# RWKV stage: the inverse's transposed copy by VectorE's 32x32 block transposes; keys, values and outputs turned as 128x128 blocks

## What is computed

```
r, k, v, z, wd, ad = split(token_shift(x @ w_in))
decay = exp(-exp(-softplus(-(w0 + tanh(wd) @ w_up)) - 0.5));  a = sigmoid(a0 + ad @ a_up)
kk = normalize(k * k_k);  k = k * (1 + (a - 1) * k_a)
for t:  sa = S @ a_t                       # a_t = -kk, b_t = kk * a
        S  = S * decay_t + sa b_t^T + v_t k_t^T
        o_t = S @ r_t
o = (o - mean(o)) * rsqrt(var(o) + eps) * gn_w + gn_b      # per head
o = (o + sum(r * k * r_k) * v) * silu(z)
```

## Time and profile before

| what | value |
|---|---|
| median of 3 runs | 3392.51 us |
| the profiled execution: its own time, its span | 3388.05 us, 3386.3 us |
| TensorE busy over the span | 97% |
| VectorE, ScalarE, GpSimd busy over the span | 47%, 21%, 62% |
| RWKV pairs: first matmul of AB of pair 1 to that of pair 8 | 93.2 us to 720.0 us: 89.5 us a pair |

### The profile page before, as it was taken

The page is one execution under the profiler, slowest core; times in us unless marked ns, Lnnn a source line. Parts: engine busy times, 40 slices in busy tenths (PEclk is TensorE's granted clock), DMA queues, the critical chain, the costliest instruction groups (busy, mean ns, idle before and its releaser), DMA issues.

```text
span 3386.3 us, 63178 instructions
## 1 busy us (share of the span) xinstructions
PE 3300.8 (97%) x21442; PEld 2638.0 (78%) x21442; DVE 1576.8 (47%) x3108; ACT 706.2 (21%) x1284; POOL 2092.9 (62%) x3460
## 2 busy tenths in 40 slices
PE   8999999999999989899999999999999999999899
PEld 6777777777788868678877777887887888888687
DVE  3455444446576763581156677223443344323500
ACT  2111111102323220140024445111121112111300
POOL 6444444446677758778763343788666666666565
PEclk9999999999999989999999999999999999999999
DMA  4111111112222213223321111333222222222232
GB/s 147 46 51 46 51 51 45 51 48 75 70 71 74 74 44 93 84 75 93 93 75 38 37 37 38 93 93 93 73 74 80 78 71 74 81 77 76 59 112 87
DMA packets 459581, 239.46 MB, mean 71 GB/s; under 512 B 27901, under 2 KB 456120, under 8 KB 458936
## 3 DMA queue, kind: packets, MB, share of 16 engines
q1 hardware_dynamic: 455656, 232.19, 23.6%
q10 hardware_dynamic: 3792, 5.28, 0.4%
HBM read 233.22 MB, written 4.19 MB: 70 GB/s over the span
## 4 chain that ended last, share of the span: by engine, by line
PE 88%; DVE 7%; ACT 2%; issue 2%; SPq 1%; DMA 0%; DVEq 0%; ACTq 0%; PEldq 0%
PE proj L338 23%; PE proj L339 21%; PE proj L340 21%; PE work L2388 2%; PE work L1136 1%; PE work L674 1%; PE work L1983 1%; PE work L688 1%; PE work L682 1%; ACT hg_tmp L1185 1%; PE work L338 1%; PE work L648 1%; PE work L340 1%; PE work L339 1%; PE work L657 1%
## 5 line engine op out<-in xcount | busy, mean ns | idle before, releaser
L314 POOL TENSOR_SCALAR w_hi<-raw_weights 128x256 fp32r<-128x256 f32 x1728 | 753.8, 462 | 1270.2 <-DMA raw_weights<-w_in 504.6
L318 POOL TENSOR_TENSOR w_lo<-raw_weights,w_hi 128x256 fp32r<-128x256 f32 x1728 | 1354.8, 814 | 0.0
L338 PE MATMUL proj<-x_hi,w_hi 128*128 128x512 f32 x2976 | 1228.1, 413 | 18.5 <-DVE x_lo L1619 6.7
L340 PE MATMUL proj<-x_hi,w_lo 128*128 128x512 f32 x2976 | 1180.8, 397 | 0.0
L339 PE MATMUL proj<-x_lo,w_hi 128*128 128x512 f32 x2976 | 1180.8, 397 | 0.0
L338 PEld LDWEIGHTS proj<-x_hi,w_hi 128*128 128x128 f32 x2976 | 562.2, 189 | 172.1 <-issue 34.5
L340 PEld LDWEIGHTS proj<-x_hi,w_lo 128*128 128x128 f32 x2976 | 561.3, 189 | 137.4
L339 PEld LDWEIGHTS proj<-x_lo,w_hi 128*128 128x128 f32 x2976 | 563.2, 189 | 117.8 <-issue 2.2
L338 PE MATMUL proj<-o_hi,w_hi 128*128 128x512 f32 x256 | 102.3, 400 | 3.7 <-DVE o_lo L1045 3.3
L339 PE MATMUL proj<-o_lo,w_hi 128*128 128x512 f32 x256 | 101.6, 397 | 0.0
L340 PE MATMUL proj<-o_hi,w_lo 128*128 128x512 f32 x256 | 101.6, 397 | 0.0
(11 more groups left out here) (470 smaller groups left out, 4226.7 us busy)
## 6 DMA issues: line engine op xcount, KB each, us to landing
raw_weights<-w_in SPq DMA_DIRECT2D x260, 256.0 KB, 3.1
raw_weights<-b_w_in SPq DMA_DIRECT2D x256, 256.0 KB, 3.1
raw_weights<-a_w_in SPq DMA_DIRECT2D x100, 256.0 KB, 3.2
raw_weights<-w_out SPq DMA_DIRECT2D x64, 256.0 KB, 3.0
raw_weights<-a_w_out SPq DMA_DIRECT2D x64, 256.0 KB, 3.0
raw_weights<-b_w_out SPq DMA_DIRECT2D x64, 256.0 KB, 3.0
raw_weights<-a_w_kv_up SPq DMA_DIRECT2D x32, 256.0 KB, 2.8
mix<-x SPq DMA_DIRECT2D x4, 1024.0 KB, 7.9
```

Of the source, the lines that this page charges most:

```text
L314: pool.tensor_scalar(part(hi_v, s, q), part(raw_v, s, q), 1.0, 1.0, ALU.mult, ALU.mult).then_inc(hi_done, 1)
L318: pool.tensor_tensor(part(lo_v, s, q), part(raw_v, s, q), part(hi_v, s, q).bitcast(F32), ALU.subtract).then_inc(w_split, 1)
L338: pe.matmul(out, w_h, a_h, start=start, stop=False)
L340: return pe.matmul(out, w_l, a_h, start=False, stop=stop)
```

## The change

Four things, in every pair:

- The turn T0 and the blocks G are gone from TensorE. VectorE instead makes `tri` as the 32x32 block transposes of `tri_t` (step T1 before the levels, and T2 to T16 after each level's X, lines 921 and 939 of the new file). Up to that point the inverse has nothing outside its 32x32 diagonal blocks. The four half-width adds of G go too.
- Bs, Vs, Ks (in this order) and `back` are turned as four 128x128 transposes each, instead of sixteen 64x64 matmuls. That leaves two quarters of each block on the other head's partitions, so ScalarE copies each turned bank out in four copies of 64x256, quarters put in place (`turn_heads`). The three turns come right behind AK, and the 3 steps and 1 step around them become 4 steps behind them.
- `back` also goes through ScalarE. VectorE's tail is two operations instead of three: scale and add the bonus in one, bias and gate in the next. The factor 0.5 moves into halved parameters.
- The shift of the next pair's V tile moves ahead of that tail, to the end of the preparation; ScalarE takes the V tile before it squares the output. VectorE's `zz` (gate) comes behind Y2, and ScalarE's `tz` behind its three turns.

```diff
-            yield 3
-            for name, src, bank, free in (("Vs", sh[:, V_], 3, "mB0"), ("Ks", k_s, 1, "mB1"), ("Bs", b_s, 0, "mK0")):
+            for name, src, bank, free in (("Bs", b_s, 0, "mK0"), ("Vs", sh[:, V_], 3, "mB0"), ("Ks", k_s, 1, "mB1")):
                 need(RW_DVE, free)
-                hold()
-                for c in range(NC_R):
-                    for hs in HEADS:
-                        mm = pe.matmul(work[bank][hs, c64(c)], src[hs, c64(c)], ident[hs, hs], start=True, stop=True)
+                for b in range(TB):
+                    mm = pe.transpose(work[bank][:, pair_cols(b)], src[:, pair_cols(b)], ident)
                 mm.then_inc(RW_PE.mark(name), 1)
-            need(RW_DVE, "tt2")
...
-            mm.then_inc(RW_PE.mark("T0"), 1)
-            yield 1
-
-            need(RW_ACT, "T0")
+            yield 4
+
+            need(RW_ACT, "Bs")
             for m in LEVELS:
-                if m > 2:
-                    need(RW_DVE, f"T{m // 2}")
+                need(RW_DVE, f"T{m // 2}")
...
-                for c in range(NC_R if m < LEVELS[-1] else 0):
-                    for hs in HEADS:
-                        even, _ = halves(y_m[hs, c64(c)], m)
-                        mm = pe.matmul(work[1][hs, c32(c)], tri_t[hs, c64(c)], even, start=True, stop=True)
...
+        def turn_heads(act, dst, bank):
+
+            for q in range(2):
+                for h in range(2):
+                    ins = act.activation(dst.rearrange("p (b q d) -> p b q d", q=2, d=64)[HEADS[h], :, q],
+                                         work[bank][:, :].rearrange("p (b h d) -> p b h d", h=2, d=64)[HEADS[q], :, h],
+                                         ACT.Copy)
+            return ins
...
+            chain()
+            done(dve.transpose(tri, tri_t), "T1")
             run(shift(dve, p, Z_, RW_DVE, "z"))
...
-            need(RW_PE, "back")
-            done(dve.tensor_scalar(g_out, work[0][:, :], p1("gn_w", p), p1("gn_b", p), ALU.mult, ALU.add), "o1")
-            chain()
-            done(dve.tensor_tensor(g_out, g_out, bonus, ALU.add), "o2")
+            need(RW_ACT, "back")
+            done(dve.scalar_tensor_tensor(g_out, g_out, h1("gn_w", p), bonus, ALU.mult, ALU.add), "o1")
```

More of the change, by code:

```diff
@@ L538, in build @@
         PR_ACT = steps("prep_act", "lora ta tw sq einc eneg eexc")
-        PR_DVE = steps("prep_dve", "d_k s_k kx d_r s_r a lw kt km L rk Lx ss " + RSQRT + " rsx K kkn kka B ends A R")
-        RW_PE = steps("rw_pe", "AB0 AB1 AK0 AK1 Vs Ks Bs T0 " + lv("Y{0} G{0} X{0}").replace(f" G{LEVELS[-1]}", "") + " " +
+        PR_DVE = steps("prep_dve", "d_k s_k kx d_r s_r a lw kt km L rk Lx ss " + RSQRT + " rsx K kkn kka B ends A R d_v s_v")
+        RW_PE = steps("rw_pe", "AB0 AB1 AK0 AK1 Bs Vs Ks " + lv("Y{0} X{0}") + " " +
                       ch("AS{0} U{0} S{0} O{0}", NC_R - 1) + " AS7 U7 O7 back")
-        RW_ACT = steps("rw_act", "tz Vs Ks Bs T0 " + " ".join(f"Sd{c}" for c in range(1, NC_R - 1)) + " gsq")
-        RW_DVE = steps("rw_dve", "d_v s_v bv mB0 mB1 mK0 mK1 tt1 tt2 d_z s_z zz " + lv("Y{0} T{0} X{0}").replace(f" T{LEVELS[-1]}", "") + " " +
+        RW_ACT = steps("rw_act", "Bs Vs Ks tz " + " ".join(f"Sd{c}" for c in range(1, NC_R - 1)) + " gsq back")
+        RW_DVE = steps("rw_dve", "bv mB0 mB1 mK0 mK1 tt1 tt2 T1 d_z s_z " +
+                       lv("Y{0} X{0} T{0}").replace("Y2", "Y2 zz").replace(f" T{LEVELS[-1]}", "") + " " +
                        ch("AS{0} U{0} S{0}", NC_R - 1) + " AS7 U7 gmean gcen gvar gvar2 " + tagged("g_") +
-                       " on o1 o2 out")
+                       " on o1 out")
         LORA_DVE = steps("lora_dve", "zero_y d s")
@@ L695, in rwkv_chunks_pe @@
             hold = lambda: pe.sem_inc(pe_waited, 1)
+            need(RW_ACT, "Ks")
             need(RW_DVE, f"X{LEVELS[-1]}")
@@ L730, in rwkv_chunks_pe @@
             need(RW_DVE, "on")
[L731 to L734, removed]
+            for b in range(TB):
+                mm = pe.transpose(work[0][:, pair_cols(b)], g_cen[:, pair_cols(b)], ident)
             mm.then_inc(RW_PE.mark("back"), 1)
@@ L755, in rwkv_act @@
                 take_tiles(i + 1, (R_, K_))
-                rwkv_chunks_act(act, i, rwkv_prep_act(act, i + 1))
-                take_tiles(i + 1, (V_, Z_))
+                for _ in rwkv_chunks_act(act, i, rwkv_prep_act(act, i + 1)):
+                    take_tiles(i + 1, (V_,))
+                take_tiles(i + 1, (Z_,))
             rwkv_within_act(act, PAIRS - 1)
-            rwkv_chunks_act(act, PAIRS - 1, iter(()))
+            run(rwkv_chunks_act(act, PAIRS - 1, iter(())))
             stage_end(act, 2, [(RW_ACT.sem, RW_ACT.after(PAIRS))])
@@ L778, in rwkv_prep_act @@
             act.activation(e_exc, e_exc, ACT.Exp).then_inc(PR_ACT.mark("eexc"), 1)
+        def turn_heads(act, dst, bank):
[5 more added lines that the diff above has]
+            return ins
         def rwkv_within_act(act, p):
             need = lambda steps, name: act.wait_ge(steps.sem, steps.done(name, p))
[L782 to L785, removed]
+            for name, dst, bank in (("Bs", b_t[:, :], 0), ("Vs", v_t[:, :], 3), ("Ks", k_t[:, :], 1)):
                 need(RW_PE, name)
-                act.activation(dst, work[bank][:, :], ACT.Copy).then_inc(RW_ACT.mark(name), 1)
+                turn_heads(act, dst, bank).then_inc(RW_ACT.mark(name), 1)
+            need(RW_DVE, "s_z")
+            act.activation(gate, sh[:, Z_], ACT.Tanh, scale=0.5).then_inc(RW_ACT.mark("tz"), 1)
         def rwkv_chunks_act(act, p, prep):
@@ L799, in rwkv_chunks_act @@
             run(prep)
+            yield
             need(RW_DVE, "gcen")
             act.activation(g_sq, g_cen, ACT.Square).then_inc(RW_ACT.mark("gsq"), 1)
+            need(RW_PE, "back")
+            turn_heads(act, g_out, 0).then_inc(RW_ACT.mark("back"), 1)
         PREP_PE_AT = (1, 3, 5, 6)
@@ L866, in rwkv_prep_dve @@
             chain()
-            done(dve.scalar_tensor_tensor(rk, sh[:, R_], p1("r_k", p), k_mod, ALU.mult, ALU.mult), "rk")
+            done(dve.scalar_tensor_tensor(rk, sh[:, R_], h1("r_k", p), k_mod, ALU.mult, ALU.mult), "rk")
             yield
@@ L898, in rwkv_prep_dve @@
             done(dve.tensor_tensor(ar[:, :, 1, :], tokens(sh[:, R_], 64), tokens(e_inc, 64), ALU.mult), "R")
+            yield
+            yield from shift(dve, p, V_, PR_DVE, "v")
         def rwkv_within_dve(dve, p):
@@ L904, in rwkv_within_dve @@
             dve.wait_ge(PR_DVE.sem, PR_DVE.after(p + 1))
-            run(shift(dve, p, V_, RW_DVE, "v"))
             need(PR_PE, "bonus")
@@ L921, in rwkv_within_dve @@
                                    repeat(c_rwkv[:, CR_EYE:CR_EYE + 64], NC_R), ALU.add), "tt2")
+            chain()
+            done(dve.transpose(tri, tri_t), "T1")
             run(shift(dve, p, Z_, RW_DVE, "z"))
-            need(RW_ACT, "tz")
-            done(dve.scalar_tensor_tensor(gate, gate, 1.0, sh[:, Z_], ALU.add, ALU.mult), "zz")
             for n, m in enumerate(LEVELS):
@@ L930, in rwkv_within_dve @@
                      f"Y{m}")
-                if m < LEVELS[-1]:
-                    need(RW_PE, f"G{m}")
-                    even, _ = halves(tri, m)
-                    chain()
-                    done(dve.tensor_tensor(even, even, work[1][:, 0:SEQ // 2].rearrange("p (x m) -> p x m", m=m),
-                                           ALU.add), f"T{m}")
+                if n == 0:
+                    need(RW_ACT, "tz")
+                    done(dve.scalar_tensor_tensor(gate, gate, 1.0, sh[:, Z_], ALU.add, ALU.mult), "zz")
                 need(RW_PE, f"X{m}")
@@ L941, in rwkv_within_dve @@
                                        ALU.add), f"X{m}")
+                if m < LEVELS[-1]:
+                    chain()
+                    done(dve.transpose(tri, tri_t), f"T{m}")
         def rwkv_chunks_dve(dve, p, prep):
@@ L986, in rwkv_chunks_dve @@
             run(prep)
-            need(RW_PE, "back")
-            done(dve.tensor_scalar(g_out, work[0][:, :], p1("gn_w", p), p1("gn_b", p), ALU.mult, ALU.add), "o1")
+            need(RW_ACT, "back")
+            done(dve.scalar_tensor_tensor(g_out, g_out, h1("gn_w", p), bonus, ALU.mult, ALU.add), "o1")
             chain()
-            done(dve.tensor_tensor(g_out, g_out, bonus, ALU.add), "o2")
-            chain()
-            done(dve.scalar_tensor_tensor(mix_v[:, bass.ds(p, 1), :].rearrange("p a t -> p (a t)"), g_out, 0.5, gate,
-                                          ALU.mult, ALU.mult), "out")
+            done(dve.scalar_tensor_tensor(mix_v[:, bass.ds(p, 1), :].rearrange("p a t -> p (a t)"), g_out, h1("gn_b", p),
+                                          gate, ALU.add, ALU.mult), "out")
         class OutStage:
```

7 lines of the change are left out of this document (1 added, 6 removed).

## The result

| | before | changed |
|---|---|---|
| median (runs) | 3392.35 us (4) | 3336.38 us (4; 3332.90 to 3338.45) |
| profiled execution, its span | 3388.05, 3386.3 us | 3332.90, 3331.1 us |
| ratio, 95% interval | | 0.9837, 0.9820 to 0.9854 |

The forecast was 3335 us, range 3329 to 3351. The page of the changed kernel, whose lines answer to the earlier trace rows: TensorE is 55 us less busy, VectorE 11 us more, ScalarE 32 us more, and TensorE's share is still 97%.

A forecast was written before the change was run, and what follows sets the result against it. TensorE, busy for 97% of the span, was taken to bound the kernel. Savings of 2.68 + 3.84 + 0.64 = 7.16 us a pair, over eight pairs 57.3 us, gave 3335 us; forecast 3330 to 3340 (0.70), wider range 3329 to 3351.

The forecast's parts named there:

- TensorE's list bounds the stage: RWKV stage: TensorE's matmuls set a pair's length; whatever leaves comes off the time unless a wait replaces it; 57.3 us.
- The turns, 2.68 us a pair: From the end of AK to Y2: 7.05 us becomes 4.37 with twelve transposes and four projection steps.
- 0.07 us wait for mK0: Ahead of Bs, the first turn: VectorE must first have read bank 0, a new wait counted in full.
- G, 3.84: Inverse levels: G blocks of 0.96 us at four levels leave TensorE, saving 3.84 us a pair.
- back, 0.64: Turn of the normalised output: 1.08 us becomes 0.44 with four transposes, saving 0.64 us a pair.
- The range's remark: In the allowance of 5 us either way: TensorE's transposes at 0.41 would make 2 us less in all.
- The transpose by VectorE, 0.69 us under a cover of 0.78: T2 to T16, between X and the next Y: up to 0.78 us costs nothing; 0.69 us was assumed.
- The rival of 1.21 us: VectorE's transpose takes 1.21 us and Y waits at 32 places: 13.8 us more, 3349 us; chance 0.12.
- the slower case: VectorE handles 32x32 blocks one by one, 2.7 us a transpose: 11 us slower than before, 3404 us; chance 0.03.
- ScalarE's quarters near 0.4 us: ScalarE's quarter copies of the turns cost nothing at 0.4 us; the rival at 0.58 gives 3345 us, chance 0.06.
- The clock rival: Twelve transposes in a row drop TensorE to 1.2 GHz from Bs to Y2: 34 us more, 3369 us; chance 0.04.
- The V shift as ScalarE's cover: VectorE's tail after back: the V shift, until about 268.9, hides ScalarE's four copies, ending by 268.0; no cost.

The follow-up runs named there:

- the parts alone: Two kernels, each with half the change: VectorE transposes with tanh moved behind ScalarE's copies, 3355.70 us; 128x128 turns with T0 and G back on TensorE, 3377.67 us.
- the last run: Changed kernel with one projection step moved ahead of back, and turns in the order Vs, Bs, Ks: 3333.37 us.
- the first form of the inverse alone: Kernel before with only T0 and G gone and VectorE's transposes in, `tz` still ahead of ScalarE's three copies: 3368.93 us against 3391.38.

## Why the prediction was right, point by point
- *TensorE's list bounds the stage.* Right: 59.5 us left the stage for 57.3 forecast, and the parts alone give the same in sum (60).
- *The turns, 2.68 us a pair.* Measured 2.81. Twelve transposes took 1.28 us (0.49, 0.43, 0.36), four steps 2.96. The term "0.07 us wait for mK0" was wrong, as the last run shows: AB to Y2 doesn't move when the first turn no longer needs mK0.
- *G, 3.84.* Measured 3.73. G was priced at 0.96 us a level, but it is 0.93: X's own block is 0.02 us longer now that it stands directly behind projection (268.89 - 267.84 = 1.05 us in the new trace; 1.03 before).
- *back, 0.64.* Measured 0.69. (The range's remark that 0.41 for each group of transposes would be "2 us less in all" is a slip: 4 x 0.03 x 8 is 1 us.)
- *The transpose by VectorE, 0.69 us under a cover of 0.78.* It takes 0.712, and the cover is 0.78: Y moved by 0.67 us with 0.75 more in the chain, and by 0.17 with 0.23. The rival of 1.21 us is out, and with it the slower case (2.7 us). The row of 1213 ns that the rival rested on was misread as a form at half pace: that same operation takes 679 ns ahead of the first pair, where GpSimd runs only a TENSOR_SCALAR beside part of it, and 1208 to 1217 ns in the other seven, where GpSimd runs TENSOR_TENSOR all the while. The estimate of 0.71 for 4-byte data, worked out from the Trainium skill's figure for a 2-byte type (VectorE: DVE Perf Modes, The three transpose paths), agrees with the trace's 0.712, and was nearer than the row of the sum of squares (685 ns).
- *ScalarE's quarters near 0.4 us.* They take 0.38 each, a turn of four 1.55. `tz` runs from 266.35 to 266.98 in the second pair, and `zz`, which needs it, starts at 267.06 behind `y_m` without a wait. The prediction listed this order only as harmless; the first form of the inverse alone shows what the old order costs there, 10 us.
- *The clock rival.* Out: the granted clock of a changed pair is 1.00.

```profile
261.00:342.00 81.00, 80.69 (x842) 60.52 (x844) 45.77 (x98) 15.38 (x35) 40.72 (x64) 1.00 0.18 52
```

- The Trainium skill says that transposes don't count as a busy TensorE in the same way for the clock (TensorE: Matmul & The Clock Gate, Part 4: PE-mode transpose). Twelve of them in 1.28 us had no effect that this row shows.
- *The V shift as ScalarE's cover.* Wrong reason, right result in seven pairs: step R of the preparation is the cover. In the eighth there is neither a V shift nor a preparation, and the copies cost about 1 us at the stage's end, which the prediction put at nothing.
- *3335 us.* That it came within 1.4 us of the measured median is luck; the four runs alone spread over 5.6 us. In the profiled executions 55.2 us went for 57.3 forecast: the stage gave 2.2 us more, the entry into HGRN took 1.3 back and a piece of lower clock near the end, with a longer wait in it, 3. The prediction gave the entry no term of its own, and it should have: a stage end gathers whoever is late. The pieces of low clock it named in its range.

## What to carry to other kernels
When one engine's list is the time, price a block as the start of the next thing less its own start, and then ask of each follower how long it may take until the next start that needs it. Here that gave a cover of 0.78 us, which a second transpose and a small copy both confirmed within some 0.02 us. And when work is taken off the bounding engine, what it waited for comes due earlier: look at the queue order of the engines behind (here one `tanh` ahead of three copies, worth 10 us) before counting the gain. Look at the last round of a loop by itself as well: what the next round's work hides is bare there. A wait that the profile puts down to an engine is only shown when moving that engine's work moves the wait.

## Not expected of the hardware
- A 128x512 transpose of 4-byte data in 32x32 blocks on VectorE takes 711 to 715 ns at all 32 places, against 0.69 us for an add of that width. It has one input, and GpSimd's work beside it does not move it; that work is mostly TENSOR_SCALAR, but one transpose had 0.51 us of GpSimd's TENSOR_TENSOR beside it and took 711 ns too.
- VectorE's 128x512 products and sums with both inputs in SBUF are another matter. In the stage before they take 0.68 to 0.93 us beside GpSimd's TENSOR_SCALAR and up to 1.22 beside its TENSOR_TENSOR (`rw_g_cen`: 691 and 1211 ns). With one input in PSUM (`tri_b`, `rw_y_m`) they take 0.69 us beside the same TENSOR_TENSOR.
- Four ScalarE copies of 64x256 from PSUM to other partitions take 0.38 us each whether or not source and destination partitions are the same (376 to 385 ns over all 128).
- The 1.6 us stop of TensorE in the eighth pair, and pieces of lower clock beside it, in some profiles and not in others.
